# The first GLU tiles of a fused decoder layer, multiplied before the RMS factor is known

## Chip, core and metric

The kernel runs on one core of a Trainium2 chip. The time is the device time of one execution, in microseconds (us). The three runs shown took 1507.45, 1507.55 and 1507.62 us. Differences are told in us against the median, 1507.55.

## What is computed

One layer over 1024 prompt tokens and 8 sample tokens (1032 columns in all), in 32-bit floats. The part that matters here stands at the very beginning: RMSNorm of the input, the input projection, and the gated unit (GLU) that feeds a causal convolution with 31 taps.

```python
def rms_norm(x, w):
    xf = x.astype(jnp.float32)
    y = xf * lax.rsqrt(jnp.mean(xf * xf, axis=-1, keepdims=True) + EPS)
    return (y * w.astype(jnp.float32)).astype(x.dtype)

def mixer(xn, ...):                      # xn = rms_norm(x, n_mix_pre)
    proj = xn @ w_in
    a_val, a_gate, q, k, v, g, gate_a, gate_b = jnp.split(proj, IN_SPLITS, axis=-1)
    u = a_val * jax.nn.sigmoid(a_gate)
    ...
    conv = lax.conv_general_dilated(full, w_dw[:, None, :], ...) + b_dw
```

After it come retention, the merge, an output projection and an MLP of width 4096. They are untouched by the change.

## The kernel before

The model dimension (1024) lies on 8 tiles of 128 partitions; the 1032 tokens lie along the free dimension, in three chunks of 344. There is no scheduler: each engine has its instructions in an order written by hand, with semaphores between engines. SP issues the weight loads; slots of 128x512 stand in a ring of four (raw), in the order of the stream wseq.

Every product is made three times to keep 32-bit precision: an operand is split into a high part (xn_h, w_h) that ScalarE (ACT in the rows) writes rounded, and a low part (xn_l, w_l), the exact difference, that VectorE (DVE) makes for x and GpSimd (POOL) makes for weights. TensorE (PE) then multiplies high by high, low by high and high by low. The function tile_mms does these three for one 128x128 tile of weights and one chunk.

The convolution needs four tiles of the GLU, and each is a pair of products: a gate group (odd number, evicted by ACT's sigmoid into sgt) and a value group (even number, evicted by DVE, which multiplies it with sgt into u_ext). So there are groups 1 to 8, G_U being 1, in four pairs. Odd groups use one set of three PSUM banks, even groups the other, banks 6 and 7 belong to the convolution. Group g may begin when group g-2 was evicted (free_set, taken).

Before the first product the tokens' factors are needed. ACT and DVE square x, DVE adds the squares of the eight k tiles down to one or two rows (sq_add, half_sum), PE sums over the partitions with a matrix of ones (x_stat), ACT makes the inverse root (x_rms, by Ln and Exp, in PSUM), DVE multiplies x in place by it (x_scale, one operand in PSUM), ACT writes the high part with the channel's gain as scale (x_hi), DVE the low part (x_lo). This is done chunk by chunk, and the first pair of groups works chunk by chunk as well (first_mms), from two pairs of weight buffers: w_h, w_l and wc_h, wc_l. Pairs 2 to 4 work over all three chunks at once, group after group (group8).

Behind it, in ACT's order, stand the sigmoids of the pairs (u_gate) and eight instructions that multiply all of x by the gains in place (x_gain), which the sums of operands for the next stage start from (x_sum on POOL). DVE works through the 124 taps of the convolution (taps) between the evictions of the four pairs and, for what is left, in the gaps of the first nine units of the next stage (units of seven products each). The four pairs end where that next stage begins.

Of the kernel before, what the change touches and what calls it, by code (L numbers as in the profile page):

```python
# [119 lines left out]
def build(nc, xT, wseq, vecs, wdwT, cacheT, s_in, rope, mask_d, ident_d,  # L120
# [8 lines left out]
    with ExitStack() as ctx:  # L129
# [60 lines left out]
        wc_h, _ = place("wc_h", [P, 2, SLOT], F32R, a_C2)  # L190
        wc_l, _ = place("wc_l", [P, 2, SLOT], F32R, a_C2 + 8 * SLOT)
# [77 lines left out]
        x0_sq = sem("x0_sq")  # L269
        fw_hi = sem("fw_hi")  # L270
# [114 lines left out]
        h_st = sem("h_st")  # L385
# [7 lines left out]
        f_st = sem("f_st")  # L393
# [15 lines left out]
        TAB_LD, CV_LD, STG_LD = 0, 64, 80  # L409
        R_X, R_LN, R_ON, R_M, R_F = 0, CHUNKS, CHUNKS + 2, CHUNKS + 14, 2 * CHUNKS + 14  # L410
# [180 lines left out]
        def _(sp):  # L591
            for i in (0, 2):
                sp.dma_start(x_in[:, 2 * i:2 * i + 2, 0:CH], xT[:, 2 * i:2 * i + 2, 0:CH]).then_inc(xa_in[i], 16)
# [3 lines left out]
            for s, n in enumerate((0, 2, 1, 3)):  # L597
                sp.dma_start(raw[:, s, :], wseq[n]).then_inc(raw_ld[s], 16)
            sp.dma_start(x_in[:, :, 2 * CH:T], xT[:, :, 2 * CH:T]).then_inc(x2_ld, 16)
            sp.dma_start(hist[:], cacheT).then_inc(hist_ld, 16)  # L600
            for n in range(RAW, 16):
                sp.wait_ge(w_split, n - RAW + 1)
                sp.dma_start(raw[:, n % RAW, :], wseq[n]).then_inc(raw_ld[n % RAW], 16)
# [223 lines left out]
        def _(pool):  # L827
# [169 lines left out]
        def _(pe):  # L997
# [3 lines left out]
            pe.sem_inc(mm, HL)  # L1001
# [37 lines left out]
            def x_stat(c, k, first, last):  # L1039

                if c < 2:
                    pe.wait_ge(x_one, 2 * c + (2 if k else 1))
                else:
                    pe.wait_ge(x_one, 4)
                out = pe.matmul(pch(G_XSTAT, c), ones[:], xsq[:, c, k * CH:(k + 1) * CH], start=first, stop=last)
                if last:
                    out.then_inc(x_st, 1)

            def first_mms(c, t, a, b):

                for k in range(a, b):
                    if c == 0 and k % SLOT_TILES == 0:
                        pe.wait_ge(w_split, t + 2 * (k // SLOT_TILES) + 1)
                    if t == 0:
                        pe.wait_ge(xn_hi, c * KT + k + 1)
                        pe.wait_ge(xn_lo, c * KT + k + 1)
                    out = tile_mms(k // SLOT_TILES, k % SLOT_TILES, XN, k, G_U + t, k == 0, k == KT - 1,
                                   (c,), (wc_h, wc_l) if t else W)
                return out

            x_stat(0, 0, True, False)
            x_stat(0, 4, False, True)
            x_stat(1, 0, True, False)
            first_mms(0, 0, 0, 3)
            pe.wait_ge(x_sq, 2)
            for k in range(4, KT):
                out = pe.matmul(pch(G_XSTAT, 1), ones[:], xsq[:, 1, k * CH:(k + 1) * CH], start=False, stop=(k == KT - 1))
            out.then_inc(x_st, 1)
            first_mms(0, 0, 3, 4)
            first_mms(0, 1, 0, 4)  # L1070
            first_mms(0, 0, 4, 8)
            first_mms(0, 1, 4, 8)
            first_mms(1, 0, 0, 4)
            first_mms(1, 1, 0, 4)
            x_stat(2, 0, True, True)
            first_mms(1, 0, 4, 8)
            first_mms(1, 1, 4, 8)
            first_mms(2, 0, 0, 4).then_inc(mm, 1)
            first_mms(2, 1, 0, 4)
            first_mms(2, 0, 4, 8).then_inc(mm, 1)  # L1080
            first_mms(2, 1, 4, 8).then_inc(mm, 2)
            with pe.Fori(0, CT - 1) as i:
                group8(G_U + 2, S_U + 4, XN, i, i * 4)
                group8(G_U + 3, S_U + 6, XN, i, i * 4)
# [364 lines left out]
            def h_stat(t):  # L1449
# [8 lines left out]
                out.then_inc(h_st, 1)  # L1458
# [8 lines left out]
            def first_half_ones():  # L1467
# [5 lines left out]
                f_ones(3, False, True, 3).then_inc(f_st, 1)  # L1473
# [11 lines left out]
            f_ones(7, False, True, BANKS[NV - 1][1]).then_inc(f_st, 1)  # L1485
# [3 lines left out]
        def _(act):  # L1489
            def rsqrt_mean(src, n, count):  # L1490
# [3 lines left out]
                return act.activation(src, src, ACT.Exp, scale=-0.5).then_inc(rms_rs, 1)  # L1494
# [4 lines left out]
            act.dma_start(vec[:], vecs).then_inc(cst_ld, 16)  # L1499
# [1635 lines left out]
```

## Time and profile before

| | |
|---|---|
| median of three runs | 1507.55 us |
| profiled execution | 1507.42 us |
| its span | 1505.5 us |
| outside the span | 1.9 us |
| PE busy | 1476.7 us (98%) |
| DVE, POOL, ACT busy | 991.4, 841.0, 650.1 us |

The span counts from the first to the last recorded instruction. A PE share of 98% says that nearly every microsecond is already matmul; what is not lies at the start and at the end. The times in rows count from the start of the span.

### The profile page before, as it was taken

What the parts mean: (1) busy time and instruction counts of PE and PEld (TensorE: products, weight loads), DVE (VectorE), ACT (ScalarE), POOL (GpSimd) and SP (SyncE); (2) the same over time, 40 slices, a digit from 0 to 9 for tenths busy, and PEclk for the clock granted to TensorE, in tenths of its full rate; (3) what the DMA queues carried; (4) which work ended last, traced back from release to release, by engine and by line L of the source; (5) the groups of instructions that cost most, each with busy time, mean ns of one, the idle gap of its engine ahead of it and who ended that gap; (6) DMA issues with size and microseconds to landing.
All of it is one profiled execution on the core that took longest, in us unless ns stands there. A gap on an engine that the chain in (4) does not pass through costs nothing.

```text
span 1505.5 us, 28469 instructions
## 1 busy us (share of the span) xinstructions
PE 1476.7 (98%) x11394; PEld 1462.6 (97%) x11394; DVE 991.4 (66%) x1245; ACT 650.1 (43%) x963; POOL 841.0 (56%) x572
## 2 busy tenths in 40 slices
PE   6999999999999999999999999999999999999996
PEld 5999999999999999999999999999999999999995
DVE  7898887757554743666714876666557756574847
ACT  6434433345554552231223765566556333332333
POOL 1467777677644662357466445555545555554555
PEclk9999999999999999999999999999999999999998
DMA  5112333422346348631232135556759575454634
GB/s 188 43 42 80 98 103 110 141 92 72 99 148 204 99 160 308 217 115 45 97 121 64 27 122 197 197 198 230 251 194 326 205 283 197 147 204 162 226 106 170
DMA packets 110091, 229.13 MB, mean 152 GB/s; under 512 B 8960, under 2 KB 20992, under 8 KB 108304
## 3 DMA queue, kind: packets, MB, share of 16 engines
q1 hardware_dynamic: 95296, 204.30, 39.3%
q10 hardware_dynamic: 14672, 23.09, 4.5%
q8 instruction: 89, 1.46, 0.4%
q14 instruction: 34, 0.28, 0.1%
HBM read 154.41 MB, written 72.95 MB: 151 GB/s over the span
## 4 chain that ended last, share of the span: by engine, by line
PE 93%; POOL 3%; issue 1%; DVE 1%; ACT 1%; DMA 1%; POOLq 0%; DVEq 0%; SPq 0%; ACTq 0%
PE ps L1441 40%; PE ps L1202 25%; PE ps L1008 16%; PE ps L1367 3%; PE ps L1354 3%; PE ps L1129 1%; PE ps L1134 1%; PE ps L1145 1%; PE ps L1131 1%; POOL w_l L841 1%; PE ps L1112 0%; PE ps L1117 0%; PE ps L1159 0%; POOL w_h L838 0%; POOL w_l L913 0%
## 5 line engine op out<-in xcount | busy, mean ns | idle before, releaser
L1441 PE MATMUL ps<-tx_h,w_h 128*128 128x258 f32 x960 | 271.5, 283 | 0.0
L1441 PE MATMUL ps<-tx_l,w_h 128*128 128x258 f32 x960 | 271.3, 283 | 0.0
L1441 PE MATMUL ps<-tx_h,w_l 128*128 128x258 f32 x960 | 271.1, 282 | 0.0
L978 POOL TENSOR_TENSOR w_l<-raw,w_h 128x512 fp32r<-128x512 f32 x120 | 185.3, 1547 | 147.2 <-ACT w_h L2027 146.7
L1441 PE MATMUL ps<-fx_l,w_h 128*128 128x258 f32 x720 | 203.7, 283 | 0.0
L1441 PE MATMUL ps<-fx_h,w_h 128*128 128x258 f32 x720 | 203.6, 283 | 0.0
L1441 PE MATMUL ps<-fx_h,w_l 128*128 128x258 f32 x720 | 203.3, 282 | 0.0
L1441 PEld LDWEIGHTS ps<-tx_h,w_h 128*128 128x128 f32 x960 | 181.4, 189 | 0.1
L1441 PEld LDWEIGHTS ps<-tx_l,w_h 128*128 128x128 f32 x960 | 181.3, 189 | 0.1
L1441 PEld LDWEIGHTS ps<-tx_h,w_l 128*128 128x128 f32 x960 | 181.2, 189 | 0.0
L2027 ACT ACTIVATE w_h<-raw 128x512 fp32r<-128x512 f32 x120 | 75.6, 631 | 186.8 <-PE ps L1441 176.5
L2311 DVE SCALAR_TENSOR_TENSOR ps<-u_ext,wdw,ps 128x512 f32<-128x512 f32 x232 | 154.8, 748 | 0.1
L978 POOL TENSOR_TENSOR w_l<-sum_y,w_h 128x512 fp32r<-128x512 f32 x60 | 92.3, 1538 | 110.5 <-ACT w_h L2027 110.5
L1441 PEld LDWEIGHTS ps<-fx_h,w_h 128*128 128x128 f32 x720 | 136.2, 189 | 0.0
L1441 PEld LDWEIGHTS ps<-fx_l,w_h 128*128 128x128 f32 x720 | 136.0, 189 | 0.0
L1441 PEld LDWEIGHTS ps<-fx_h,w_l 128*128 128x128 f32 x720 | 135.9, 189 | 0.0
L1202 PE MATMUL ps<-xn_h,w_h 128*128 128x258 f32 x416 | 119.7, 288 | 0.0
L1202 PE MATMUL ps<-xn_l,w_h 128*128 128x258 f32 x416 | 117.5, 282 | 0.0
L1202 PE MATMUL ps<-xn_h,w_l 128*128 128x258 f32 x416 | 117.4, 282 | 0.0
L2865 DVE TENSOR_TENSOR fac<-ps,fac 128x516 f32<-128x516 f32 x79 | 54.5, 690 | 83.4 <-PE ps L1441 83.4
L913 POOL TENSOR_TENSOR w_l<-raw,w_h 128x512 fp32r<-128x512 f32 x54 | 74.5, 1380 | 55.0 <-ACT w_h L1628 54.8
L838 POOL TENSOR_TENSOR w_h<-raw,zero 128x512 fp32r<-128x512 f32 x36 | 39.8, 1106 | 115.9 <-PE ps L1145 54.7
(384 smaller groups left out, 4333.0 us busy)
## 6 DMA issues: line engine op xcount, KB each, us to landing
raw<-wseq_dram SPq DMA_DIRECT2D x264, 256.0 KB, 3.0
quad_scratch<-quad_h SPq DMA_DIRECT2D x16, 774.0 KB, 3.5
tx_h<-quad_scratch SPq DMA_DIRECT2D x12, 1032.0 KB, 10.3
tx_l<-hidden_scratch SPq DMA_DIRECT2D x12, 1032.0 KB, 12.7
gate_scratch<-gst SPq DMA_DIRECT2D x10, 1032.0 KB, 5.0
hidden_scratch<-hq_g SPq DMA_DIRECT2D x8, 1032.0 KB, 6.9
hidden_scratch<-stg_b SPq DMA_DIRECT2D x6, 1032.0 KB, 6.9
hq_g<-hidden_scratch SPq DMA_DIRECT2D x6, 1032.0 KB, 13.4
```

Of the source, the lines that this page charges most:

```text
L838: pool.tensor_tensor(hi, raw[:, s, :], zero[:, 0:1].broadcast_to([P, SLOT]), ALU.add).then_inc(w_hi, 1)
L841: pool.tensor_tensor(lo, raw[:, s, :], hi.bitcast(F32), ALU.subtract).then_inc(w_split, 1)
L913: pool.tensor_tensor(lo, src, hi.bitcast(F32), ALU.subtract).then_inc(xw_lo, 1)
L978: pool.tensor_tensor(lo, src, hi.bitcast(F32), ALU.subtract).then_inc(q_lo, 1)
L1008: out = pe.matmul(pch(g, c), w[a][:, place_, sub * P:(sub + 1) * P], xs[b][:, k, c * CH:(c + 1) * CH], start=(first and n == 0), stop=(las ...
L1202: out = pe.matmul(ps[:, 2 * n + s, 0:HC], XRINGS[q % RING][wa][:, kk * P:(kk + 1) * P], x_operand(i, xb, kk, s), start=(i < 3 and kk == 0 ...
L1354: out = pe.matmul(pch(g, m), (wo_h, wo_l)[a][:, slot, sub * P:(sub + 1) * P], MG[b][:, k, c * CH:(c + 1) * CH], start=(k == 0 and n == 0), ...
L1367: out = pe.matmul(pch(g, c), DIRECT_W[slot][a][:, (k % SLOT_TILES) * P:(k % SLOT_TILES + 1) * P], FX[b][:, k, c * CH:(c + 1) * CH], start= ...
L1441: out = pe.matmul(ps[:, 2 * n + s, 0:HC], RINGS[q % RING][wa][:, kk * P:(kk + 1) * P], OPS[x][xb][:, QK * kh + kk, at_:at_ + HC], start=(i ...
L2027: act.activation(RINGS[q % RING][0], src, ACT.Copy).then_inc(q_hi, 1)
L2311: out = dve.scalar_tensor_tensor(dst, u_, w_, bank, ALU.mult, ALU.add)
L2865: dve.tensor_tensor(dst, pair(n), dst, ALU.add).then_inc(ev_d, 1)
```

## The change

The first pair of groups is multiplied with x that has its gains but not the token's factor: x_hi and x_lo work on the loaded x at once. Its eviction multiplies by the factor: DVE writes both groups, chunk by chunk, times rr into SBUF (u_rows), and ACT's sigmoid and DVE's product then work from there. The factors rr are kept in SBUF. The second pair works chunk by chunk too, from the same four weight buffers, with x normalised as before. So x is split twice: x_hi and x_lo run for six chunk passes and not three (numbers 0 to 2 unnormalised, 3 to 5 normalised, the latter by x_norm_hi). x_scale takes its factor from SBUF. The adding of squares for chunks 1 and 2 goes from DVE to POOL (square_add). Weight loads come earlier in SP's order, and the first eight slots go through first_hi and first_lo. In ACT's order the eight x_gain instructions wait for all six passes. The taps are spread anew.

```diff
@@ SP
-            for i in (0, 2):
-                sp.dma_start(x_in[:, 2 * i:2 * i + 2, 0:CH], xT[:, 2 * i:2 * i + 2, 0:CH]).then_inc(xa_in[i], 16)
+            sp.dma_start(x_in[:, 0:2, 0:CH], xT[:, 0:2, 0:CH]).then_inc(xa_in[0], 16)
+            sp.dma_start(raw[:, 0, :], wseq[FIRST[0]]).then_inc(raw_ld[0], 16)
+            sp.dma_start(x_in[:, 4:6, 0:CH], xT[:, 4:6, 0:CH]).then_inc(xa_in[2], 16)
+            for s in range(1, RAW):
+                sp.dma_start(raw[:, s, :], wseq[FIRST[s]]).then_inc(raw_ld[s], 16)
...
@@ POOL
+            def square_add(c, half):
+                q = xsq[:, c, :].rearrange("p (k n) -> p k n", k=KT)
+                if half < 2:
+                    pool.wait_ge(x_sq, 2 * (c - 1) + half + 1)
+                    a = q[:, 4 * half:4 * half + 2]
+                    pool.tensor_tensor(a, a, q[:, 4 * half + 2:4 * half + 4], ALU.add).then_inc(x_one, 1)
+                else:
+                    pool.wait_ge(x_one, 3 * c + 1)
+                    pool.tensor_tensor(q[:, 0:2], q[:, 0:2], q[:, 4:6], ALU.add).then_inc(x_one, 1)
...
@@ PE
+            for c in range(CHUNKS):
+                for half in range(2):
+                    for t in range(2):
+                        first_mms(0, c, t, half).then_inc(u_mm, 1)
+                if c < 2:
+                    x_stat(c)
+            for c in range(2):
+                for half in range(2):
+                    for t in range(2):
+                        first_mms(1, c, t, half)
+                    if c == 0 and half == 0:
+                        x_stat(2)
+            for t in range(2):
+                for half in range(2):
+                    first_mms(1, 2, t, half).then_inc(mm, 1)
@@ ACT
             def first_hi(s):
-                act.wait_ge(raw_ld[s], 16)
+                act.wait_ge(raw_ld[s % RAW], 16 * (s // RAW + 1))
+                if s >= RAW:
+                    act.wait_ge(u_mm, 8 + s - RAW + 1)
+            def x_norm_hi(c, half):
+                act.wait_ge(u_mm, 4 * c + 4)
+                act.wait_ge(x_sc, 2 * c + half + 1)
+                x_hi(c, 4 * half, 4 * half + 4)
...
-            weight_hi(4)
             u_gate(0)
-            weight_hi(5)
-            act.wait_ge(xn_lo, CHUNKS * KT)
+            x_norm_hi(2, 0)
+            x_norm_hi(2, 1)
+            act.wait_ge(xn_lo, 2 * CHUNKS * KT)
             for k in range(KT):
                 x_gain(k)
-            weight_hi(6)
-            weight_hi(7)
+                if k == 3:
+                    weight_hi(8)
             u_gate(1)
@@ DVE
+            def u_rows(c):
+                cs = slice(c * CH, (c + 1) * CH)
+                for t, rows in enumerate((sgt, u_ext[:, 0, HIST:HIST + T])):
+                    dve.wait_ge(u_mm, 4 * c + 3 + t)
+                    dve.tensor_tensor(rows[:, cs], pch(G_U + t, c), rr[:, cs], ALU.mult).then_inc(u_fr, 1)
...
             u_out(0)
             u_sample(0)
-            taps(14)
+            taps(4)
             u_out(1)
             u_sample(1)
-            taps(14)
+            taps(13)
@@ DVE, units of the next stage
                     if j == 1:
                         taps(4 if v < 4 else 5)
+                    if j == 5 and v >= 4:
+                        taps(1)
                     if j == 6:
-                        taps(5 if v < 4 else 6)
+                        taps(6)
```

On DVE, where chunks 1 and 2 are scaled and split, the order before was this (sgt, ps, rr, x_in and so on are the tiles named above; ps is PSUM):

```order
L2263 TENSOR_TENSOR x_in<-x_in,ps 128x4x344 [waits rms_rs,dve_c]
L2263 TENSOR_TENSOR x_in<-x_in,ps 128x4x344
L2271 SCALAR_TENSOR_TENSOR xn_l<-x_in,vec,xn_h 128x344 [waits xn_hi] x4
L2237 TENSOR_TENSOR xsq<-xsq 128x688 [waits x_sq]
L2237 TENSOR_TENSOR xsq<-xsq 128x344 [waits dve_c]
L2290 TENSOR_TENSOR xsq<-xsq 128x344 [waits dve_c]
L2271 SCALAR_TENSOR_TENSOR xn_l<-x_in,vec,xn_h 128x344 [waits xn_hi] x4
```

Now the same engine has this, from the eviction of chunk 0 of the first pair to that of chunk 1:

```order
L2312 TENSOR_TENSOR sgt<-ps,rr 128x344 [waits u_mm,rms_rs]
L2312 TENSOR_TENSOR u_ext<-ps,rr 128x344 [waits u_mm]
L2295 TENSOR_TENSOR x_in<-x_in,rr 128x4x344 x2
L2304 SCALAR_TENSOR_TENSOR xn_l<-x_in,vec,xn_h 128x344 [waits xn_hi] x12
L2295 TENSOR_TENSOR x_in<-x_in,rr 128x4x344 [waits rms_rs]
L2304 SCALAR_TENSOR_TENSOR xn_l<-x_in,vec,xn_h 128x344 [waits xn_hi] x4
L2295 TENSOR_TENSOR x_in<-x_in,rr 128x4x344
L2312 TENSOR_TENSOR sgt<-ps,rr 128x344 [waits u_mm]
L2312 TENSOR_TENSOR u_ext<-ps,rr 128x344 [waits u_mm]
```

The factor of x_scale moved from PSUM (ps) to SBUF (rr), the low parts became twice as many, and the adds of squares left. They stand on POOL now, among the low parts of the first weights:

```order
L855 TENSOR_TENSOR wc_l<-raw,wc_h 128x512 [waits fw_hi]
L864 TENSOR_TENSOR xsq<-xsq 128x688 [waits x_sq,x_one]
L864 TENSOR_TENSOR xsq<-xsq 128x688 [waits x_sq]
L867 TENSOR_TENSOR xsq<-xsq 128x688 [waits x_one]
L864 TENSOR_TENSOR xsq<-xsq 128x688 [waits x_sq]
L855 TENSOR_TENSOR w_l<-raw,w_h 128x512 [waits fw_hi]
L864 TENSOR_TENSOR xsq<-xsq 128x688 [waits x_sq]
L867 TENSOR_TENSOR xsq<-xsq 128x688 [waits x_one]
L855 TENSOR_TENSOR wc_l<-raw,wc_h 128x512 [waits fw_hi]
L855 TENSOR_TENSOR w_l<-raw,w_h 128x512 [waits fw_hi]
```

Before, POOL had four low parts of weights in this stretch and nothing else. On ACT, around the gains, the order was this:

```order
L1572 ACTIVATE sgt<-ps 128x1032 [waits mm]
L1564 ACTIVATE w_h<-raw 128x512 [waits mm,raw_ld1]
L1576 ACTIVATE x_in<-x_in,vec 128x1032 [waits xn_lo]
L1576 ACTIVATE x_in<-x_in,vec 128x1032 x7
L1564 ACTIVATE w_h<-raw 128x512 [waits mm,raw_ld2]
L1564 ACTIVATE w_h<-raw 128x512 [waits mm,raw_ld3]
L1572 ACTIVATE sgt<-ps 128x1032 [waits ps_free0,mm]
```

Now it is this, beginning with the sigmoid of pair 1, which works in SBUF:

```order
L1615 ACTIVATE sgt<-sgt 128x1032 [waits u_fr]
L1557 ACTIVATE xn_h<-x_in,vec 128x344 [waits x_sc,u_mm]
L1557 ACTIVATE xn_h<-x_in,vec 128x344 x3
L1557 ACTIVATE xn_h<-x_in,vec 128x344 [waits x_sc,u_mm]
L1557 ACTIVATE xn_h<-x_in,vec 128x344 x3
L1626 ACTIVATE x_in<-x_in,vec 128x1032 [waits xn_lo]
L1626 ACTIVATE x_in<-x_in,vec 128x1032 x3
L1608 ACTIVATE w_h<-raw 128x512 [waits mm,raw_ld0]
L1626 ACTIVATE x_in<-x_in,vec 128x1032 x4
L1622 ACTIVATE sgt<-ps 128x1032 [waits c_init,mm]
```

The eight gains keep their place between the sigmoids of pair 1 and pair 2, but their wait is now for the low parts of the third chunk of pair 2 and not of pair 1.

## Rows read from the trace of the kernel before

**Rows 1.** The page: busy time, and the chain that ended last.
```profile
PE 1476.7 (98%) x11394; PEld 1462.6 (97%) x11394; DVE 991.4 (66%) x1245; ACT 650.1 (43%) x963; POOL 841.0 (56%) x572
...
PE 93%; POOL 3%; issue 1%; DVE 1%; ACT 1%; DMA 1%; POOLq 0%; DVEq 0%; SPq 0%; ACTq 0%
```

**Rows 2.** Chain of waits, 0 to 90 us: start, length, what.
```profile
15.37 2.92 PE ps L1008 x9
18.29 3.88 PE ps L1067 x8
22.16 9.95 PE ps L1008 x63
32.11 0.59 PE ps L1045 x2
...
37.47 52.63 PE ps L1008 x332
```

**Rows 3.** Timeline of DVE from 28 us: start, length, engine, line, operation, tiles.
```profile
33.75 3.08 DVE L2263 TENSOR_TENSOR x_in<-x_in,ps 128x1376 f32<-128x1376 f32 x2 [0.54 <-ACT ps L1494]
36.76 3.98 DVE L2271 SCALAR_TENSOR_TENSOR xn_l<-x_in,vec,xn_h 128x344 fp32r<-128x344 f32 x8
45.51 1.23 DVE L2336 TENSOR_TENSOR u_ext<-ps,sgt 128x1032 f32<-128x1032 f32 x1 [4.77 <-PE ps L1008]
...
68.04 1.23 DVE L2336 TENSOR_TENSOR u_ext<-ps,sgt 128x1032 f32<-128x1032 f32 x1 [1.37 <-PE ps L1008]
```

**Rows 4.** Timeline of ACT from 28 us, the gains and the second sigmoid.
```profile
35.38 3.90 ACT L1535 ACTIVATE xn_h<-x_in,vec 128x344 fp32r<-128x344 f32 x8 [1.66 <-DVE x_in L2263]
...
44.90 8.48 ACT L1576 ACTIVATE x_in<-x_in,vec 128x1032 f32<-128x1032 f32 x8
53.28 0.62 ACT L1564 ACTIVATE w_h<-raw 128x512 fp32r<-128x512 f32 x1
...
57.27 1.02 ACT L1572 ACTIVATE sgt<-ps 128x1032 f32<-128x1032 f32 x1
```

**Rows 5.** Timeline of POOL, 12 to 24 us, and its first sum of operands.
```profile
13.58 1.27 POOL L847 TENSOR_TENSOR w_l<-raw,w_h 128x512 fp32r<-128x512 f32 x1 [12.74 <-ACT w_h L1521]
...
18.56 1.56 POOL L847 TENSOR_TENSOR w_l<-raw,w_h 128x512 fp32r<-128x512 f32 x1
20.73 1.38 POOL L847 TENSOR_TENSOR wc_l<-raw,wc_h 128x512 fp32r<-128x512 f32 x1 [0.61 <-ACT wc_h L1521]
...
58.69 2.42 POOL L868 TENSOR_TENSOR sx<-x_in 128x1032 f32<-128x1032 f32 x1
```

**Rows 6.** Timeline of DVE in the same stretch, single instructions.
```profile
13.00 1.65 DVE L2263 TENSOR_TENSOR x_in<-x_in,ps 128x688 f32<-128x688 f32 x2 [0.36 <-ACT ps L1494]
...
18.90 1.58 DVE L2271 SCALAR_TENSOR_TENSOR xn_l<-x_in,vec,xn_h 128x344 fp32r<-128x344 f32 x1
...
20.90 1.58 DVE L2271 SCALAR_TENSOR_TENSOR xn_l<-x_in,vec,xn_h 128x344 fp32r<-128x344 f32 x1
```

**Rows 7.** Groups by line, 12 to 68 us: count | busy us, mean ns of one | idle before.
```profile
L1511 ACT ACTIVATE xsq<-x_in 128x1376 f32<-128x1376 f32 x3 | 4.0, 1337 | 0.0
...
L2237 DVE TENSOR_TENSOR xsq<-xsq 128x688 f32<-128x688 f32 x3 | 2.6, 868 | 1.0 <-ACT xsq L1511 1.0
...
L1492 ACT ACTIVATE ps<-ps,eps_b 128x344 f32<-128x344 f32 x3 | 1.6, 522 | 3.9 <-PE ps L1045 3.6 <-PE ps L1067 0.3
L2237 DVE TENSOR_TENSOR xsq<-xsq 128x344 f32<-128x344 f32 x3 | 1.6, 518 | 0.1
...
L1494 ACT ACTIVATE ps<-ps 128x344 f32<-128x344 f32 x3 | 1.3, 442 | 0.1
```

**Rows 8.** Timeline of ACT to 10 us: when parts of x had landed.
```profile
5.18 0.78 ACT L1511 ACTIVATE xsq<-x_in 128x688 f32<-128x688 f32 x1 [2.10 <-DMA x_in<-xT_dram]
...
6.97 0.78 ACT L1511 ACTIVATE xsq<-x_in 128x688 f32<-128x688 f32 x1 [1.01 <-DMA x_in<-xT_dram]
```

**Rows 9.** Stretches: start:end, length, busy time, PEclk, DMA share, GB/s.
```profile
5.00:8.00 3.00, 0.00 (x0) 0.00 (x0) 2.28 (x4) 1.55 (x2) 0.00 (x0) 1.00 1.09 373
...
1491.40:1495.00 3.60, 0.00 (x0) 0.00 (x0) 3.50 (x6) 1.77 (x3) 3.52 (x4) 1.00 0.58 220
1495.00:1496.00 1.00, 0.00 (x0) 0.00 (x0) 1.00 (x3) 0.00 (x0) 0.92 (x2) 0.93 0.56 208
1496.00:1500.00 4.00, 0.00 (x0) 0.00 (x0) 4.00 (x8) 0.00 (x0) 3.92 (x4) 0.50 0.87 327
```

**Rows 10.** Timeline of PE: two matmuls early, two later.
```profile
15.79 0.49 PE L1008 MATMUL ps<-xn_l,w_h 128*128 128x344 f32 x1
...
16.08 0.49 PE L1008 MATMUL ps<-xn_h,w_l 128*128 128x344 f32 x1
...
22.47 0.32 PE L1008 MATMUL ps<-xn_h,wc_h 128*128 128x344 f32 x1
...
22.63 0.32 PE L1008 MATMUL ps<-xn_l,wc_h 128*128 128x344 f32 x1
```

**Rows 11.** DVE's busy time in units of 19.8 us of the next stage.
```profile
153.00:172.80 19.80, 15.80 (x23) 1.00 0.31 100
...
192.60:212.40 19.80, 16.89 (x26) 1.00 0.25 87
```

More of the change, by code:

```diff
@@ L1038, in _, with x_stat @@
             pe.wait_ge(c_init, 1)
[L1039 to L1053, printed above, removed]
+            def x_stat(c):
+                pe.wait_ge(x_one, 3 * c + 2)
+                if c == 2:
+                    pe.wait_ge(rms_rs, 1)
+                for n, k in enumerate((0, 1) if c else (0, 4)):
+                    out = pe.matmul(ps[:, 6 + c % 2, 0:CH], ones[:], xsq[:, c, k * CH:(k + 1) * CH],
+                                    start=(n == 0), stop=(n == 1))
+                out.then_inc(x_st, 1)
@@ L1058, in first_mms @@
                                    (c,), (wc_h, wc_l) if t else W)
                 return out
[L1061 to L1069, printed above, removed]
@@ L1457, in h_stat @@
                                     start=True, stop=True)
-                out.then_inc(h_st, 1)
+                out.then_inc(x_st, 1)
             def f_ones(row, first, last, n):
@@ L1472, in first_half_ones @@
                 pe.wait_ge(f_sq, 8)
[L1473 removed]
+                f_ones(3, False, True, 3).then_inc(x_st, 1)
             for v in range(NV):
@@ L1538, in _ @@
+            act.wait_ge(xa_in[1], 16)
+            x_hi(0, 2, 4)
+            act.wait_ge(xa_in[2], 16)
+            x_hi(0, 4, 6)
+            first_hi(1)
+            act.wait_ge(xa_in[3], 16)
+            x_hi(0, 6, 8)
+            first_hi(2)
+            first_hi(3)
             x_square(0, 0, 2, xa_in[0], x0_sq)
             x_square(0, 4, 6, xa_in[2], x0_sq)
-            x_square(1, 0, 4, xb_in[0], x_sq)
+            for i in range(2):
+                act.wait_ge(xb_in[i], 16)
+                x_hi(1, 4 * i, 4 * i + 4)
@@ L2056, in h_root @@
             def h_root(t):
-                act.wait_ge(h_st, t + 1)
+                act.wait_ge(x_st, CHUNKS + t + 1)
                 act.activation(two(hms[:, HALVES[t]]), pair(3), ACT.Square,
@@ new lines, in _ @@
+                sq_add(2 * i - 2, 1).then_inc(x_one, 1)
+            x_lo(1, 0, 8)
+            dve.wait_ge(rms_rs, R_X + 1)
+            u_rows(0)
+            x_scale(0, 0)
+            x_scale(0, 1)
+            x_lo(2, 0, 8)
+            x_lo(3, 0, 4)
+            dve.wait_ge(rms_rs, R_X + 2)
+            x_scale(1, 0)
+            x_lo(3, 4, 8)
+            x_scale(1, 1)
+            u_rows(1)
+            x_lo(4, 0, 4)
+            dve.wait_ge(rms_rs, R_X + 3)
+            x_scale(2, 0)
+            u_rows(2)
@@ L2294, in _ @@
+            x_lo(4, 4, 8)
+            x_scale(2, 1)
+            x_lo(5, 0, 8)
             HALF = SEQ // 2
@@ L2933, in root_argument @@
             def root_argument(t, n):
-                dve.wait_ge(f_st, t + 1)
+                dve.wait_ge(x_st, CHUNKS + 2 + t + 1)
                 dve.wait_ge(h_cp, t + 1)
```

212 lines of the change are left out of this document (104 added, 108 removed).

## The prediction

> **What bounds the kernel now.** I read the page first: PE is busy for 98% of the span and is 93% of the chain that ended last [rows 1]. So time can only be won or lost where PE does not multiply, and the change touches only the start. The chain of waits shows that start in five pieces [rows 2]: the first product at 15.37, a 3.9 us block of ones matmuls, one more of 0.59 us, a hole until 37.47, and from there PE without a gap. Groups 1 and 2 end at 45.5 and groups 3 and 4 at 68.0, where DVE evicts them at once [rows 3]. So a pair costs PE 22.5 us, or 0.157 us for each of its 144 matmuls. Two pairs are 45.0 us of the 68.0; the other 23.0 are start, statistics, the hole and a slow clock. From group 5 on I take everything to follow PE, so the whole forecast is: when can group 5 start, against 68.0?
>
> **What the change removes.** PE no longer waits for the factors. The first quarter of chunk 0 had landed at 5.2 and the third at 7.0 [rows 8], at 373 GB/s [rows 9]. The first weights come behind one piece of x, with another queue's piece between: about 0.26 MB to 0.5 MB more, so 6.7. High part 0.6, low part 1.3 [rows 4, 5]: PE can start at about 8.8, 6.6 us earlier. It also loses the hole (1.2) and part of the ones matmuls: four, in the slow stretch, and one fast become six fast ones at 0.59, 3.5 us. If nothing else stopped PE, two pairs would end near 58, 10 us earlier. What follows asks who stops it.
>
> **The walk through the new order.** Single costs: low part of x 0.49 each in a row, x_scale 1.5 each [rows 3]; high part of x 0.49 each [rows 4]; squares 1.34, adds 0.87 and 0.52, Ln 0.52, Exp 0.44 [rows 7]. DVE makes the eight low parts of chunk 0 as ACT delivers them, among its weights, until 14.1, then the squares and adds of chunk 0, two times 0.87 + 0.87 + 0.52 with small waits: 19.0. PE has finished chunk 0 by then (24 tiles, the first six us at half rate: 19). Two ones matmuls, 1.2: the sum stands at 20.6. ACT: root 1.0, two squares of chunk 1 2.6, eight high parts of chunk 2 3.9, two squares 2.6: until 30.7.
>
> At this point POOL and DVE meet. The rows show what that costs: a low part of x took 1.58 us, not 0.57, twice, both times behind a POOL instruction that ran already [rows 5, 6]. So 1.0 us was lost to a POOL instruction of 1.3 us. POOL's own grew to 1.56 and 1.38 as it waited in turn. An x_scale with its factor in PSUM ran beside POOL at 13.6 and took its normal 1.65 for two [rows 5, 6]. The change moves x_scale's factor to SBUF, doubles the low parts and puts six adds and four low parts of weights on POOL in the same stretch. An add of 688 columns lies between POOL's 1.29 for 512 and 2.42 for 1032 [rows 5]: 1.67, of which 1.4 holds DVE.
> POOL can add chunk 1 from 23.0. Its three adds alternate with two x_scales of 1.5: 23.0 + 3 x 1.4 + 2 x 1.5 + 0.3 = 30.5. PE ended chunk 1 at 28.0 and waits for this sum, then has 1.2 of ones and a first low part that stood behind POOL, so its first quarter of chunk 2 (1.9) ends at 34.4. That frees a weight buffer: ACT goes on with 0.5 + 1.0 + 2.0 (weights, root, four high parts). DVE makes the four low parts of pass 3 between POOL's two adds and three low parts: from 36.6 to 42.3, where alone they took 2.0. From 42.3 DVE has no idle time left: one POOL part 1.0, four x_scales 6.0, twenty low parts 9.8, four evictions of pair 1 at 0.44 (estimate from the 0.52 add) 1.8, another POOL part 0.9: **61.8** for the last low part. Here the gains begin, since they wait for all six passes: ACT 8.5 + 0.5 + 1.0 until the second sigmoid ends [rows 4]: 61.8 + 10.1 = 71.9, and with the step to PE **72.2**. PE ended pair 2 at 66.5; it stands for 5.7 us, since group 5 needs group 3's banks and the sigmoid that frees them stands behind the eight gains. Before, that sigmoid was done at 58.3, ten us early [rows 4]. So 72.2 - 68.0 = **+4.2 us**.
>
> The Trainium skill has the rule for the collision, in "SBUF — State Buffer", Who interferes with whom: an instruction of VectorE with two SBUF inputs and one of GpSimd that reads SBUF lock each other out, and one with at most one SBUF input does not contend. The trace agrees, by the 1.58 and the undisturbed 1.65. It speaks against this change in two places, x_scale's operand and the moved adds.
>
> **The clock.** The first matmuls are 0.29 apart, those from 22 us on 0.16 [rows 10], which for 344 columns are 1.2 and 2.4 GHz; the slow stretch lasted from 15.4 to about 21, so 5.6 us of which half, 2.8, is lost. (The granted clock is printed as 1.00 there; the spacing decides.) At the end of the kernel PE stood from 1491.4, and the granted clock fell to 0.50 after 4.5 us of that [rows 9]. A stall of 5.7 us is longer. So I expect that group 5 starts at 1.2 GHz. The cost is between nothing and 2.8; I take 2.0. The Trainium skill, "TensorE: Matmul & The Clock Gate", Why this matters for your kernels, advises against idle gaps between bursts of matmuls, since the array falls back to its slow clock. The row at the end agrees; no stall in the middle of this trace is long enough to show it.
>
> **The rest.** Slots 4 to 7 are loaded long before 31, so nothing waits for them. The operand sums on POOL start at 71 and not at 58.7; they move with the gains, 13 us later against a PE that is 4 later. Eight sums and eight low parts are 8 x 2.4 + 8 x 1.3 = 30 us in the 45 us of pairs 3 and 4; hidden, and with that cover gone 1 us for each us late. DVE has 26 taps behind it at the next stage and not 37; units get one tap more, 1.3 us on 15.8 to 16.9 of 19.8 [rows 11]: it still fits, nothing on the path; at most 1 us where an eviction is late. The semaphores that were merged (h_st, f_st into x_st) issue nothing else. Sum: profiled time 1507.4 + 4.2 + 2.0 = 1513.6. The median lies 0.1 above the profiled time, so **1513.8**.
>
> **Rivals.**
> A, the clock stays up: 1507.5 + 4.2 = 1511.8. For it: 4.5 us of idle at the end went by before it fell, and 5.7 is not much more.
> B, no collisions of weight, faster: if DVE and POOL overlap freely, the same walk has the sum of chunk 1 at 28.0, the last low part at 53.0, the second sigmoid at 63.1 and group 5 at 63.4, with PE waiting 2.8: -4.6, so 1503.0. What decides is the time of the last low part: the sign turns where it comes at 57.6 (68.0 less 0.3 and 10.1). Against it are the two rows of 1.58. For it: only two such events are to be seen, none with x_scale from SBUF.
> C, collisions, but fewer, because POOL's adds fall into DVE's waits or ACT runs ahead of my walk: last low part near 57.5, 1507.5, no change. This also stands for a start of PE earlier than 8.8, since a start moved by 1 us moves everything behind it by 1 us.
> D, more is late than I see: x's pieces land 1 to 2 us later because weights go in between, or evictions in the units are late: 1516 to 1517.
>
> **Numbers.** Forecast case 0.42, A 0.22, B 0.14, C 0.13, D 0.09. A difference under 0.2% (3.0 us) can hardly be told from no change in this kernel. The range takes the forecast, A, C and the near part of D: 1506.0 to 1516.2. Faster is B and a little of C: 0.17. Slower than 1510.6 is the forecast, A and D less a little: 0.68. Same: 0.15.
>
> **What would show it.** PE's first product near 9; the ones matmul of chunk 1 waiting for POOL's add near 30; low parts of x of 1.6 to 2.0 us in length behind POOL, and an x_scale of over 2.5 us near 24; the last low part near 62; the eight gains at 62 to 71, the sigmoid of pair 2 at 71, and PE's longest wait, over 5 us, on that sigmoid, with matmuls 0.22 apart (258 columns) or 0.29 (344) behind it if the clock fell. The prediction is wrong if x_scale from SBUF runs at 1.5 beside POOL, if the last low part comes before 57.6, or if PE waits anew in the units behind 120 us.

## The result and the profile after

The changed kernel takes 1516.67 us (median of six runs, 1515.67 to 1518.56), the kernel before in the same comparison 1507.58 (1507.45 to 1507.91). The ratio is 1.0059, 95% interval 1.0049 to 1.0070: slower by 9 us. The forecast was 1513.8 with 1506.0 to 1516.2 as its range, so the sign was right and the time lies 0.5 us above the range. The profiled execution took 1516.57 us, its span is 1514.5 against 1505.5, and these 9.0 us are what has to be found.

The page of the changed kernel, busy time and chain, against [rows 1]:

```profile
PE 1479.5 (98%) x11390; PEld 1467.6 (97%) x11390; DVE 1015.8 (67%) x1267; ACT 661.0 (44%) x987; POOL 853.3 (56%) x578
...
PE 92%; POOL 3%; ACT 2%; DVE 1%; issue 1%; DMA 1%; POOLq 0%; SPq 0%; DVEq 0%; ACTq 0%
```

The page alone says little: PE's busy time grew by 2.8 us with four matmul records fewer, a first hint at a slower clock, and ACT is now 2% of the chain. PE's waits, the view that names them (waited for, us in total, times, longest):

```profile
PE ps L1041 <- POOL w_l L855: 7.3, 1, 7.3
PE ps L1041 <- ACT sgt L1622: 4.3, 1, 4.3
PE ps L1078 <- POOL xsq L867: 2.6, 1, 2.6
PE ps L1041 <- DVE xn_l L2304: 1.6, 2, 0.8
...
PE ps L1231 <- POOL w_l L946: 1.2, 2, 1.1
PE ps L1231 <- DVE gst L2641: 0.8, 1, 0.8
```

The first is the start, 8.1 us earlier than the 15.37 of [rows 2]. The second and third are the two stops in the start that the prediction walked to. The last two are new and lie near 220 us, far behind the change. The chain of waits from 0 to 90 us shows how the start hangs together:

```profile
21.87 4.67 POOL xsq L864 x2
26.60 2.88 POOL xsq L867
29.53 2.00 PE ps L1078 x4
...
36.56 6.93 DVE xn_l L2304 x4
...
66.88 4.19 ACT x_in L1626 x4
71.06 0.92 ACT sgt L1622
```

GpSimd's adds of squares, VectorE's low parts and ScalarE's gains with the sigmoid behind them are on the path, and TensorE stands. VectorE's timeline has the two numbers on which the prediction hung:

```profile
22.56 5.42 DVE L2295 TENSOR_TENSOR x_in<-x_in,rr 128x1376 f32<-128x1376 f32 x2
...
58.04 3.98 DVE L2304 SCALAR_TENSOR_TENSOR xn_l<-x_in,vec,xn_h 128x344 fp32r<-128x344 f32 x8
...
120.50 1.23 DVE L2391 TENSOR_TENSOR u_ext<-ps,sgt 128x1032 f32<-128x1032 f32 x1 [0.26 <-PE ps L1041]
```

Two scalings of x take 5.42 us, where before the change two took 3.08 [rows 3], and the last low part ends at 62.0 (forecast: 61.8). The third row is the end of pair 4; before it stood at 113.50. So the start and the pairs cost 7.0 us. Group 5 began at 72.1 against 68.0, which is 4.1 of them. The stretches show where 2.9 went (start:end, length, busy times, PEclk):

```profile
30.00:31.00 1.00, 1.00 (x5) 0.67 (x3) 1.00 (x1) 0.00 (x0) 1.00 (x1) 0.62 0.00 0
31.00:32.00 1.00, 1.00 (x4) 0.76 (x4) 1.00 (x2) 0.00 (x0) 0.34 (x1) 0.50 0.00 0
...
44.00:45.00 1.00, 1.00 (x6) 1.00 (x5) 1.00 (x1) 0.00 (x0) 0.62 (x1) 0.50 0.81 209
...
71.00:72.00 1.00, 0.00 (x0) 0.00 (x0) 0.00 (x0) 1.00 (x3) 0.86 (x1) 0.60 0.00 0
72.00:78.00 6.00, 5.89 (x20) 5.90 (x21) 5.78 (x7) 0.49 (x1) 6.00 (x4) 0.50 0.01 3
```

The granted clock fell near 71, while TensorE stood, and stayed at 0.50 (1.2 GHz) until 78: 5.9 us of multiplying at half rate, half of it lost, 2.95. And it fell twice before: near 30.2, behind the 2.6 us wait for the sum of chunk 1, until 33.7, and near 43.9, behind two waits of 0.8 us for VectorE's low parts with three matmuls between them, until about 47.3. Neither stretch was in the forecast. The first is on the path. The second is not: VectorE works without a gap from 36.6 to the last low part, and in the run with the load ahead of the store, where the clock stayed up at both places, the last low part ended at 61.1, which is the 0.9 us earlier that its first quarter of chunk 2 had brought. What the slow stretches do is let TensorE end pair 2 later, at 67.8, so that the stall on the sigmoid is 4.3 us (5.2 in that run).

The last 2.0 us are lost at 219 to 230, in the fifth unit of the next stage. There VectorE multiplies a gate (gst), SP stores it and then loads the unit's fourth slot of weights, and GpSimd sums with it. The same place before the change first, VectorE, GpSimd, ScalarE and SP:

```profile
200.57 0.69 DVE L2579 TENSOR_TENSOR gst<-ps,gst 128x516 f32<-128x516 f32 x1 [1.32 <-PE ps L1202]
...
207.76 2.37 DVE L2513 TENSOR_TENSOR gst<-gst,sgm 128x1032 f32<-128x1032 f32 x2
207.75 3.54 POOL L913 TENSOR_TENSOR wx_l<-wx_y,wx_h 128x512 fp32r<-128x512 f32 x1 [1.58 <-ACT wx_h L1628]
206.55 0.60 ACT L1850 ACTIVATE gst<-ps 128x516 f32<-128x516 f32 x1 [1.76 <-PE ps L1202]
210.58 0.47 SPq L623 DMA_DIRECT2D raw<-wseq_dram  x1
```

and in the changed kernel:

```profile
207.47 0.69 DVE L2635 TENSOR_TENSOR gst<-ps,gst 128x516 f32<-128x516 f32 x1
...
214.65 4.37 DVE L2568 TENSOR_TENSOR gst<-gst,sgm 128x1032 f32<-128x1032 f32 x2
214.41 1.29 POOL L946 TENSOR_TENSOR wx_l<-wx_y,wx_h 128x512 fp32r<-128x512 f32 x1 [1.58 <-ACT wx_h L1678]
213.21 0.60 ACT L1900 ACTIVATE gst<-ps 128x516 f32<-128x516 f32 x1 [1.76 <-PE ps L1231]
219.47 0.47 SPq L629 DMA_DIRECT2D raw<-wseq_dram  x1
...
224.31 1.29 POOL L921 TENSOR_TENSOR wx_x<-raw 128x512 f32<-128x512 f32 x1 [4.15 <-DMA raw<-wseq_dram]
```

Measured from the first row of each, VectorE comes to its gate products after 7.19 and 7.18 us, the same. GpSimd comes to its low part after 7.18 before (a tie within 0.01 us, which VectorE won) and 6.94 now, since TensorE reached the eviction that ScalarE waits for after 5.98 before and 5.74 now. So before, VectorE had its gate products done in 2.37 us and GpSimd's low part stretched to 3.54; now GpSimd is there 0.24 us ahead, and VectorE's stretch to 4.37. The load stands behind the gate's store on SP; it is issued 10.0 us after the first row before, and 12.0 us now. GpSimd then waits 4.15 us for it, and TensorE 1.9 us, 1.1 for a low part and 0.8 for an eviction. The sum of the three parts is 4.1 + 2.9 + 2.0 = 9.0, the difference of the spans.

### The profile page after: what moved, and what is told of

Its sections match the earlier page's. It is cut to its first block, busy times and chain, and to the rows that moved or that the text cites. A ratio compares the mean times of both kernels' runs of the same rounds, so it can differ in the third digit from the quotient of the medians.

```text
span 1514.5 us, 28526 instructions
## 1 busy us (share of the span) xinstructions
PE 1479.5 (98%) x11390; PEld 1467.6 (97%) x11390; DVE 1015.8 (67%) x1267; ACT 661.0 (44%) x987; POOL 853.3 (56%) x578
## 4 chain that ended last, share of the span: by engine, by line
PE 92%; POOL 3%; ACT 2%; DVE 1%; issue 1%; DMA 1%; POOLq 0%; SPq 0%; DVEq 0%; ACTq 0%
PE ps L1470 40%; PE ps L1231 25%; PE ps L1041 14%; PE ps L1396 3%; PE ps L1383 3%; PE ps L1158 1%; PE ps L1163 1%; PE ps L1174 1%; PE ps L1160 1%; DVE xn_l L2304 1%; POOL w_l L847 1%; PE ps L1141 0%; PE ps L1146 0%; PE ps L1188 0%; ACT x_in L1626 0%
```

## Experiments

Each kernel differs from the changed one (1516.67) by what its diff shows, unless its heading names another kernel that it starts from; "..." marks lines of a diff that are left out. All were timed against the kernel before, which stood at 1507.5 to 1507.7 throughout.

**Keep TensorE busy in the stall.** Fourteen unread ones matmuls between pair 2 and group 5.

```diff
-                    first_mms(1, 2, t, half).then_inc(mm, 1)
+                    out = first_mms(1, 2, t, half)
+                    if t and half:
+                        for _ in range(14):
+                            out = pe.matmul(ps[:, 0, CH:CH + 160], ones[:], xsq[:, 1, 0:160], start=True, stop=True)
+                    out.then_inc(mm, 1)
```

> Fourteen ones matmuls of 160 columns, whose result nobody reads, follow the last product of pair 2, so TensorE is busy for some 4 us of its stall of 4.3 us. Theory (the clock term): group 5 starts at the same 72.1 us, but at 2.4 GHz: matmuls 0.157 us apart from the first, and 2.9 us less than the changed kernel in all, 1513.7. Rival (the slow spacing after the stall is a start-up of the weight and operand reads, or contention at 72 to 78 us, and not the clock): the matmuls are 0.29 us apart all the same and the time stays at 1516.6.

Measured: 1515.34 (1513.36 to 1515.73), ratio 1.0043 (1.0029 to 1.0056). The stretches of its trace, the last of them the one that had 0.50 above:

```profile
66.00:72.00 6.00, 6.00 (x43) 5.93 (x42) 4.49 (x7) 6.00 (x7) 1.59 (x2) 1.00 0.17 46
72.00:78.00 6.00, 5.50 (x36) 5.33 (x35) 5.22 (x6) 1.06 (x2) 6.00 (x4) 1.00 0.00 0
```

The clock stayed at 1.00, and 36 matmul records stand in six microseconds where there were 20. From the start of group 5 to the end of pair 4 the trace has 45.8 us instead of 48.4, 2.6 less. This execution began 0.5 us later, though (first product 7.7), waited 0.4 more near 220, and the median gained only 1.3. The mechanism is shown by the clock column; the size in the median is half of what was expected. The five executions fall in two groups: 1513.36 and 1514.02 with a mean granted clock of 0.997, and 1515.34 to 1515.73 with 0.994. The profiled one is of the second group, and in it the clock fell at 31.0 and again at 44.8, where these matmuls do nothing.

**Five taps in the fourth unit.**

```diff
-                        taps(6)
+                        taps(5 if v == 3 else 6)
```

> Unit 3 gets five taps and not six on VectorE, so unit 4 begins with less behind it. Theory (unit 4 is full: VectorE's 19.80 of 19.80 us, so its gate products lose the race for SBUF to GpSimd, and the raw load stands behind the late gate store on SP's queue): TensorE's waits of 1.1 and 0.8 us near 220 us go, the load is issued some 6 us earlier, and the time falls by 2.0 to 1514.6. Rival (the load is late because SP's queue was filled in another order, whatever VectorE does): the waits stay, 1516.6. Second rival: the tap that is left over makes a later unit full, and the wait comes back there: between 1515 and 1516.6.

Measured: 1516.69 (1515.70 to 1517.09), no change. VectorE was now idle for 1.21 us ahead of the first row of the comparison above, and yet its gate products took 4.39 us, GpSimd's wait was 4.14, and TensorE's 1.1 and 0.8 stood as before. So my theory that the fifth unit was full is out. What remains is the 0.24 us by which GpSimd comes first, which does not depend on VectorE's load but on when TensorE reaches an eviction.

**The sigmoid ahead of the last four gains.**

```diff
-                low_part(n % RAW, n)
+                if n != 2 * RAW + 1:
+                    low_part(n % RAW, n)
                 if n == 2 * RAW:
+                    low_part(n % RAW + 1, n + 1)
...
                 if k == 3:
                     weight_hi(8)
-            u_gate(1)
-            weight_hi(9)
+                    u_gate(1)
+                    weight_hi(9)
```

> The sigmoid of pair 2 and the next high part of weights are moved on ScalarE from behind the eighth gain to behind the fourth, and both low parts of weights on GpSimd ahead of its operand sums. Theory (group 5 waits for the sigmoid that stands behind eight gains, and nothing else): the sigmoid ends at 68.0 and not 72.0, the stall of 4.3 us goes to under 1 us, the clock does not fall, so group 5 starts 3.8 us earlier and 2.9 us of slow clock are saved: 6.7 less, 1510; less what the operand sums, now later, take back from pairs 3 and 4. Rival (the stall is only moved: the high parts and sums behind it become late and TensorE waits in groups 6 to 8 instead): the start of group 5 at 68, but a wait of 2 to 4 us between 75 and 90, 1513 to 1515.

Measured: 1513.40 (1512.22 to 1513.66), ratio 1.0032. The sigmoid ended at 67.8, group 5 began at 68.3, the clock stayed up. But pair 4 ended at 116.57, not 120.50: of 6.7 us, 2.8 were given back. TensorE's waits say to whom:

```profile
PE ps L1043 <- POOL w_l L885: 2.2, 4, 1.1
```

GpSimd's operand sums wait for the last gain in any case, and low parts of weights stand behind them. A new wait of 1.2 us for an eviction came at 135 us as well. The stall went as the theory had it, but the time lies where the rival had put it.

**The adds of squares back on VectorE.**

```diff
-            pool.wait_ge(x_one, 2)
-            for half in range(3):
-                square_add(1, half)
-            square_add(2, 0)
...
             x_scale(0, 1)
+            square_adds(1)
             x_lo(2, 0, 8)
+            square_adds(2)
             x_lo(3, 0, 4)
```

> The six adds of squares of chunks 1 and 2 go back from GpSimd to VectorE. Theory (GpSimd's adds and VectorE's x_scale lock each other out of SBUF, which costs VectorE more than the adds themselves would): although VectorE has 4.5 us more to do, its x_scale falls from 2.7 to 1.5 us each and the last low part of x comes at about 59.4 and not 62.0; group 5 starts 2.6 us earlier, the stall before it shrinks to about 2 to 4 us, and the time is 1514.0, or 1511 if the shorter stall keeps the clock up. Rival (no collision of weight; VectorE simply has more work): the last low part comes 3 to 4.5 us later, at 65 to 66, and the time is 1520.

Measured: 1512.47 (1511.32 to 1513.81), ratio 1.0029 (1.0020 to 1.0038). VectorE has more to do and is done sooner. Its timeline:

```profile
23.23 3.08 DVE L2288 TENSOR_TENSOR x_in<-x_in,rr 128x1376 f32<-128x1376 f32 x2
```

Two scalings take 3.08 again and not 5.42. The last low part ended at 58.7 (62.0) and group 5 began at 68.8, 3.3 us earlier. TensorE waited only 1.3 us for the sum of chunk 1, and no slow stretch followed there. The stall was longer, 5.2 us, since TensorE ended pair 2 earlier too, and the clock fell in it. The rival, "VectorE simply has more work", is out.

**The factor read from PSUM.**

```diff
...
+                act.activation(rr[:, c * CH:(c + 1) * CH], src, ACT.Exp, scale=-0.5).then_inc(rms_ln, 1)
+                act.wait_ge(rms_ln, 2 * c + 2)
+                act.activation(src, src, ACT.Exp, scale=-0.5).then_inc(rms_rs, 1)
...
-                dve.tensor_tensor(xs, xs, rr[:, c * CH:(c + 1) * CH].unsqueeze(1).broadcast_to([P, 4, CH]), ALU.mult
+                dve.tensor_tensor(xs, xs, ps[:, 6 + c % 2, 0:CH].unsqueeze(1).broadcast_to([P, 4, CH]), ALU.mult
```

> VectorE's scaling of x reads the factors from PSUM, as before the change, and the copy in SBUF is made for the evictions alone (one more Exp of 0.44 us on ScalarE for each chunk). The adds of squares stay on GpSimd. Theory (each scaling with two SBUF inputs and each add on GpSimd lock each other out): the two scalings of chunk 0 take 1.5 and not 2.7 us, GpSimd's adds run beside them, the last low part of x comes 2 to 3 us earlier, near 59.5, and the time is 1513.7. Rival (the lock is among low parts of x and GpSimd, the scalings only queue behind them): last low part within 1 us of 62, time 1516 to 1517.

Measured: 1511.69 (1510.82 to 1512.56), ratio 1.0023. VectorE's and GpSimd's rows:

```profile
22.49 3.08 DVE L2300 TENSOR_TENSOR x_in<-x_in,ps 128x1376 f32<-128x1376 f32 x2
...
22.29 3.32 POOL L864 TENSOR_TENSOR xsq<-xsq 128x688 f32<-128x688 f32 x2 [8.90 <-ACT xsq L1540]
```

The same instruction, beside the same adds, takes 1.5 us with one operand in PSUM and 2.7 with both in SBUF, and the two adds take 3.32 and not 4.66. That isolates the collision. The gain was 5.0 us and not 2.9: the sum of chunk 1 came 1.9 us earlier, TensorE waited 0.8 for it and not 2.6, and the slow stretch near 31 us was gone. The last low part ended at 57.8 (59.5 forecast) and group 5 began at 67.9. The clock fell at 40.4, behind waits of 0.4, 0.8 and 0.8 us, and in the stall, where the slow stretch took 1.4 us from the two pairs and not 2.6.

**The load ahead of the gate's store,** in SP's order of each unit.

```diff
-                if v - 2 in X_GATES:
-                    gate_store(v - 2)
                 sp.wait_ge(xw_lo, STEPS * (v - 1) + 6)
                 sp.dma_start(raw[:, 3, :], wseq[n + 3]).then_inc(raw_ld[3], 16)
+                if v - 2 in X_GATES:
+                    gate_store(v - 2)
```

> In the changed kernel each unit's fourth load of weights is issued on SP ahead of the gate store and not behind it. Theory (the 2.0 us of unit 4 are lost because the gate products on VectorE lost the race for SBUF to GpSimd by 0.24 us, ended 2 us later, and the load stands behind their store): the load is issued near 215.8 and not at 219.5, GpSimd's idle time of 4.15 us before its sum goes, TensorE's waits of 1.1 and 0.8 us near 220 go, though the gate products still take 4.4 us; the time is 1514.7. Rival (TensorE waits there for GpSimd's work and not for the load): waits stay, 1516.6.

Measured: 1513.42 (1512.76 to 1514.04), ratio 1.0035. GpSimd's and SP's rows:

```profile
218.41 1.29 POOL L921 TENSOR_TENSOR wx_x<-raw 128x512 f32<-128x512 f32 x1
...
211.14 0.33 SPq L627 DMA_DIRECT2D raw<-wseq_dram  x1
217.34 0.38 SPq L653 DMA_DIRECT2D gate_scratch<-gst  x1
```

The gate products still took 4.37 us, but the load went out 6.2 us ahead of the store, GpSimd had no idle time ahead of its sum, and the wait of 1.1 us was gone. The wait of 0.8 for VectorE's eviction stayed, which I had expected to go. Fetching the load early is worth more than the 1.1, because a second wait for GpSimd, at 230 us, is gone too, and the starts of matmuls show both as longer than the view prints them: gaps of 1.4 and 0.5 us where 0.12 is the rule. From the end of pair 4 to the end of the span it is 2.1 us less. The rest of the 3.25 us is in a start that this edit does not touch: group 5 began at 71.2 and pair 4 ended at 118.85, 1.65 us earlier. Its stretches show why:

```profile
30.00:31.00 1.00, 1.00 (x6) 0.70 (x5) 1.00 (x1) 0.00 (x0) 1.00 (x1) 1.00 0.00 0
...
68.00:69.00 1.00, 0.00 (x0) 0.00 (x0) 0.98 (x2) 1.00 (x3) 0.00 (x0) 0.82 0.62 82
```

The same program up to there, the same wait of 2.6 us, and no fall of the clock near 30; and at the stall it fell near 68.6 and not near 71.2, so less of the slow stretch fell on matmuls.

**The same exchange in the kernel before.**

> The same exchange of load and store in the kernel before. Theory (there the gate products won the race, took 2.4 us and the load was in time): no change, 1507.3 to 1507.7, with 0.2 us less wait near 221 at best. Rival (the store delays the loads in every unit, in both kernels): 1505.5 to 1506.5.

Measured: 1507.71 (1507.42 to 1508.23), ratio 0.9998. No change, and the trace holds an answer to another question:

```profile
207.89 4.38 DVE L2513 TENSOR_TENSOR gst<-gst,sgm 128x1032 f32<-128x1032 f32 x2
207.66 1.29 POOL L913 TENSOR_TENSOR wx_l<-wx_y,wx_h 128x512 fp32r<-128x512 f32 x1 [1.58 <-ACT wx_h L1628]
```

In the kernel before, with nothing changed but SP's order, the race for SBUF now goes the other way as well: GpSimd comes 0.23 us first and VectorE's products take 4.38. So who wins is decided by tenths of a microsecond of earlier waits, and losing it cost 2.0 us only where the load stood behind it.

**All four edits together** (adds on VectorE, factor from PSUM, sigmoid ahead, load ahead).

> Adds on VectorE, factors read from PSUM, the sigmoid of pair 2 behind the fourth gain, and the load ahead of the store, in one kernel. Theory: last low part near 58.3, sigmoid at 64, TensorE waits about 1 us and keeps its clock, group 5 starts near 64.3 (68.0 before the change); of the 3.7 us some 2.8 are given back in pairs 3 and 4 to GpSimd's late sums, as in the experiment with the moved sigmoid; no wait in unit 4: 1504 to 1506.6. Rival (the sums on GpSimd, which start behind the last gain, take back all of it): 1507.5 to 1509.

Measured: 1506.68 (1505.10 to 1507.67), ratio 0.9990 (0.9981 to 0.9999). Group 5 began at 63.4, 4.6 us ahead of the kernel before, with the clock up; pair 4 ended at 111.69 against 113.50. PE's waits:

```profile
PE ps L1036 <- POOL w_l L878: 3.1, 4, 1.4
PE ps L1226 <- DVE gst L2653: 2.0, 2, 1.2
```

It is the only version whose interval lies below the kernel before, by 1 us, which is less than what I said could be told. What an early group 5 wins is mostly given back to GpSimd's sums, and 1.2 us of it at 130 us, in a wait for an eviction that the kernel before does not have.

**TensorE busy in both waits,** on top of the load ahead of the store: the fourteen as above, and nine more before the sum of chunk 1.

```diff
+                if c == 1:
+                    for _ in range(9):
+                        pe.matmul(ps[:, 7, CH:CH + 160], ones[:], xsq[:, 0, 0:160], start=True, stop=True)
                 if c < 2:
                     x_stat(c)
```

> The kernel with the load ahead of the store, and TensorE kept busy with unread ones matmuls in both of its waits: nine in the 2.6 us before the sum of chunk 1 (27 to 29.5 us), fourteen in the stall before group 5. Theory (the clock falls in both waits, in the first in some executions and not in others, which is why the same start gave group 5 at 71.1 and at 72.1 us): matmuls 0.157 us apart all the way from the end of the first slow stretch; last low part at 61, group 5 at 71, no slow stretch behind it, and executions closer together: 1510 to 1510.8. Rival (the second slow stretch, near 31 us, comes from something else than the wait, contention of the weight loads for instance): it stays in some executions, and only the 2.9 us behind the stall are saved: 1510.5 to 1511.5 with the same spread.

Measured: 1511.43 (1510.92 to 1511.71), 2.0 us less than the version without the matmuls. The nine executions lie within 0.8 us (1.3 in the five without, 2.9 in the six of the changed kernel), and behind neither wait is there a clock under 1.00. Group 5 began at 71.2 as in that version, whose profiled execution had no slow stretch near 31 either, so only the second was saved there: pair 4 ended at 116.92 and not 118.85. The time is 0.6 above the range that I gave and inside the rival's, so the time does not decide between them. What speaks for the theory is the smaller spread and that all nine executions have a mean granted clock of 0.996 or 0.997, as the kernel before has. No pair of traces with and without the nine matmuls shows that the first wait alone brings on the first slow stretch.

**Low parts ahead of sums, and taps moved.** Both on top of all four edits.

```diff
-                if n < 15:
-                    x_sum(n - 2 * RAW + 1)
+                for i in {10: (1, 2), 11: (3,), 12: (4, 5), 13: (6,), 14: (7,)}.get(n, ()):
+                    x_sum(i)
...
             weight_hi(10)
+            weight_hi(11)
             x_operand_hi(2)
-            weight_hi(11)
```

> The combined kernel, with GpSimd's operand sums one place further back: low part 10 stands behind one sum and not three, low part 11 behind three and not four, and ScalarE's high part 11 ahead of its operand. Theory (what the earlier start of group 5 wins is given back because a low part of weights stands behind three sums that begin only after the last gain): TensorE's waits of 3.1 us in groups 6 to 8 fall to under 1 us, pairs 3 and 4 end near 109.5 and not 111.7, and the time is 1504 to 1505. Rival (VectorE is the bound at 112 to 130 us, where it has two operand low parts of 3.4 us each and eight taps): pairs 3 and 4 end earlier but TensorE waits as much longer for the eviction near 130 us, and the time stays at 1506 to 1507.

Measured: 1507.49 (1505.74 to 1508.09), in the median no better than the 1506.68. The executions fall in two groups: four at 1505.7 to 1506.1 with a mean granted clock of 0.996 or 0.997, and seven at 1507.1 to 1508.1 with 0.995. The profiled one (1505.75) is of the first. Its chain of waits:

```profile
84.17 4.74 POOL x_in L899 x2
88.97 1.81 issue
90.78 0.62 ACT w_h L1608
91.47 1.99 POOL w_l L878
```

The waits of 3.1 us in four pieces became 3.2 in two: TensorE no longer waits at 76 and 82, but ScalarE makes an operand out of the sums (the 1.81), and the next high part of weights stands behind that. The theory named the right chain and the wrong link.

In the next run three taps were moved as well:

```diff
-            taps(13)
+            taps(14)
...
-            taps(9)
+            taps(11)
...
-                        taps(4 if v < 4 else 5)
+                        taps(1 if v == 0 else 4 if v < 4 else 5)
```

> As the run before, and three of VectorE's taps moved from the first unit to ahead of groups 5 to 8, where it was idle for 3.5 and 4.5 us. Theory: TensorE's wait of 1.2 us at 130 us goes as well: 1503 to 1504. Rival (VectorE's idle time there is gone once TensorE waits less, so the taps delay the evictions of groups 7 and 8): no better than the run before.

Measured: 1506.37 (1505.19 to 1507.26), ratio 0.9990 (0.9981 to 1.0000). The wait of 1.2 us at 130 went, as expected, and the median fell by 1.1; the time expected was missed by 2 us. The 3.2 stayed, and the profiled execution (1507.26, the slowest of the eleven) shows what the second of its two waits can do:

```profile
94.45 0.74 PE L1036 MATMUL ps<-xn_h,w_h 128*128 128x344 f32 x3 [1.85 <-POOL w_l L878]
...
95.00:96.00 1.00, 1.00 (x7) 1.00 (x6) 1.00 (x3) 0.00 (x0) 1.00 (x1) 0.64 0.37 88
96.00:97.00 1.00, 1.00 (x5) 1.00 (x4) 1.00 (x2) 0.00 (x0) 1.00 (x2) 0.50 0.47 174
```

Behind a wait of 1.85 us the clock fell near 95.3 and stayed down until 98.7, which took 1.7 us. In the run before, the same wait (1.84) passed with the clock at 1.00 in the execution that was profiled. The two groups of that kernel's executions lie about as far apart, so putting four short waits together into two longer ones probably costs a slow stretch in most executions; this is an inference, since no trace of its slower group was kept.

## Why the prediction was right and where it failed

**The start.** The mechanism and its size held. Last low part 61.8 forecast, 62.0 measured; group 5 at +4.2 forecast, +4.1 measured; the gains and then the sigmoid on the path, and the longest wait of TensorE on that sigmoid. Two edits that take the collision away by different means, one by moving the adds, one by moving an operand, gained 4.2 and 5.0 us. A scaling cost 2.7 us beside the adds, as 1.5 plus 1.2 (the forecast had 1.4 for that). Some agreement is luck: the first product came at 7.3 and not 8.8, and the slow stretch near 31 us, about 1 us, took that back. TensorE ended pair 2 at 67.8 and not 66.5, so its stop before group 5 was 4.3 us and not 5.7; the start of group 5 did not depend on that. Rival B falls with the row of 5.42. The Trainium skill, "SBUF — State Buffer", Who interferes with whom, says that a VectorE instruction with at most one SBUF input, outside the engine's 2-port modes, does not contend with GpSimd; the run with the factor in PSUM agrees, by 1.5 against 2.7 us.

**The clock.** "The cost is between nothing and 2.8; I take 2.0": it was 2.9 in the profiled execution (2.6 by the run that kept TensorE busy), because multiplying began when the clock had just fallen and nearly the whole slow stretch fell on it. This term was sized 0.9 too small. The forecast was a mean between the ends although I held that the clock would fall, and then the whole slow stretch of the start, 2.8, was the value. Rival A falls with the column of 0.50, and the run that kept TensorE busy shows that the wait caused it.

**The rest.** The step that failed is "units get one tap more, 1.3 us on 15.8 to 16.9 of 19.8 [rows 11]: it still fits, nothing on the path; at most 1 us where an eviction is late". It was 2.0 us, in one unit, and so the prediction's own sign of being wrong, that PE waits anew behind 120 us, came true. The tap ahead of it was not the cause, as the run with five taps shows; the busy share said nothing either. The cause was a race for SBUF of 0.24 us, followed by a store and a load in one queue. Rival D named late evictions in the units and gave 1516 to 1517, where the time came out; its chance was 0.09. To see it ahead one would have had to look at the two rows at 207.75 and 207.76, where GpSimd's low part took 3.54 us and not 1.29, and ask what happens if VectorE comes second. With 0.9 more for the clock and 2.0 for the race the forecast's 1513.8 would have been 1516.7.

**What stays open.** Why TensorE reaches the eviction 0.24 us sooner relative to VectorE in the changed kernel: the trace before has a gap of that length at 200.4, behind a low part that ended at 200.4 too, and no run takes that gap away alone. Open is also what makes the clock fall in one execution and not in the next. The experiments ran on three chips (the first four, the next four and the last three of them), so between two traces the chip can differ too; but the executions of one kernel on one chip fall in two groups as well.

## What to carry to other kernels

A VectorE instruction with two inputs in SBUF and a GpSimd instruction that works in SBUF were not parallel work here (2.7 us against 1.5); before moving an operand from PSUM to SBUF or adds to the other engine, count what then stands beside what. A wait of TensorE as long as those here (1.85, 2.6 and 4.3 us) can cost more than its length: add the slow stretch behind it, or fill it, and do not gather short waits into a long one unseen. And where a load stands behind a store in one queue, the load inherits every lateness of the store's producer; look for such pairs far behind the change as well.

## What the runs showed of the hardware

The same program with the same wait gave different clocks. Behind the wait of 2.6 us before the sum of chunk 1 the clock fell in the changed kernel and in three more of the traces with the same start (at 30.1 to 31.0), and stayed up in that with the load ahead of the store. At the stall it fell near 71.2 in the changed kernel and near 68.6 in the one with the load ahead. The first rise came when multiplying had gone on for 5.9 us in the first (7.3 to 13.1) and for 3.4 in the second (7.2 to 10.6), by the spacing of matmuls. The Trainium skill, "TensorE: Matmul & The Clock Gate", What's actually happening, says that the number of slow matmuls at the start of one kernel differs from run to run; these two traces agree, with 20 and 11. A wait need not be long: the clock fell behind one of 1.85 us, and behind two of 0.8 with three matmuls between them. So the moment depends on something that the program does not set, and executions of one kernel differ by 1 to 2 us where it can fall, while those with TensorE kept busy lie within 0.8. A price of such a fall is a range. Behind the first wait it was about 1 us. Behind the stall it was 1.4 us (factor from PSUM), 1.9 (load ahead of the store) and 2.6 to 2.7 (the changed kernel, five taps, adds on VectorE), by the time from the start of group 5 to the end of pair 4 against the 45.8 us with the clock up.
